# The causal mask of an attention stage: an addition by VectorE, or a product added on TensorE

## The chip, the cores and the metric

The kernel runs on one core of a Trainium2 chip. The metric is the device time of one execution in microseconds (us), taken as the median over several runs. The engines are named as the profile names them: PE is TensorE's matrix multiplication, PEld its weight load, DVE is VectorE, ACT is ScalarE, POOL is GpSimd, and SP is the engine that only issues transfers here. They run side by side and wait for each other through semaphores.

## What is computed

The program is two transformer blocks over 1024 positions of width 1024. The first has a retention and an RWKV mixer and a mixture of 32 experts, the second a latent attention, a short convolution, a state space mixer and a gated feed-forward layer. The change touches only the attention of the second block. Cut to that, the reference is

```python
def block(i):                                   # 128 queries, i = 0..7
    start = i * Q_BLOCK
    sc = jnp.einsum("bqhd,bkhd->bhqk", qn, k_nope) + jnp.einsum("bqhd,bkd->bhqk", qr, k_rope)
    sc = sc.astype(jnp.float32) * scale
    causal = (start + jnp.arange(Q_BLOCK))[:, None] >= key_idx[None, :]
    p = jax.nn.softmax(jnp.where(causal, sc, -jnp.inf), axis=-1)
    return jnp.einsum("bqhk,bkhd->bqhd", p.astype(v.dtype), v)
```

with 8 heads, queries and keys of 96 elements (64 and 32 rotary ones), and values of 64. All of it is float32.

## The kernel before

The program is a row of stages. Each stage has an instruction list of its own for every engine, written out by hand, and ends in a barrier of all engines. `attention_stage` stands between the mixers' stage and the feed-forward stage.

A **step** m is one head and one block i of 128 queries, against the i + 1 blocks of keys that it may see. There are 64 steps. Four steps make a group: the small block i and the large block 7 - i, for each of two heads (u = 0, 1), in the order small u0, large u0, small u1, large u1. Four groups (i = 0 to 3) finish a pair of heads, and the stage has 16 groups. A small step has 1 to 4 blocks of keys, a large one 5 to 8.

In each step:

- PE makes the scores (line 3270) into PSUM: one product of up to 512 columns for a small step, two for a large one. In a profile each float32 product is two records, one for each pass.
- DVE adds the mask `future` (0, and -1e30 right of the diagonal) to the last 128 columns of the scores, in place (line 3358), takes the largest of each row (line 3362), and makes the bias of the exponential from it (line 3366).
- ACT takes the exponential and its sum (line 3323).
- PE turns the result block by block (line 3278, with the identity `ident`; one record each), into the same PSUM banks.
- DVE (small, line 3373) or ACT (large, line 3331) copies the turned blocks to SBUF. After that the banks are free for the scores four steps later.

For each pair of steps of a class, DVE takes the reciprocal of the sums (line 3379), POOL spreads it (line 3259), PE turns it (line 3286), ACT copies that (line 3338), PE multiplies by the values (line 3296, two heads side by side in the array), and DVE multiplies both (line 3385).

PE's order is written out: at step m it makes `scores(m + 2)`, then, where m % 4 is 0 (large class) or 3 (small class), `turn_shares`, then `turn(m)`, and then at those same steps `weigh`. PE waits for the bank in `scores`, for the exponential in `turn`, and for ACT's copy in `weigh`. DVE's order at step m is `shares_of` (m % 4 of 2 or 3), `bound(m + 2)`, `small_out`, `finish`. ACT's order is the copy of the shares, `exps(m + 1)`, and `large_out(m)` for a large step.

The mask comes by a transfer of 64 KB, the first that SP issues in the stage (line 3248). Semaphore `const` tells of it, and DVE waits for it ahead of its first step. `ident` has been in SBUF since the program's start.

Of the kernel before, what the change touches and what calls it, by code (L numbers as in the profile page):

```python
# [10 lines left out]
ALU = mybir.AluOpType  # L11
# [4 lines left out]
P = 128  # L16
# [4 lines left out]
BANK = 512  # L21
# [82 lines left out]
def three(ap, a):  # L104
    return ap.rearrange("p (a b) -> p a b", a=a)
# [2303 lines left out]
def wide(psum, b, n):  # L2409

    return psum[:, b:b + n, :].rearrange("p a b -> p (a b)")
# [780 lines left out]
def attention_stage(nc, psum, bank, ident, a, q_t, k_t, values, feat, late):  # L3192
# [14 lines left out]
    with Stage(nc, "attention") as st:  # L3207
        future = st.sb("future", [P, P])
# [3 lines left out]
        total, share = ([st.sb(f"{n}{c}", [P, 2]) for c in range(2)] for n in ("total", "share"))  # L3212
        spread = [st.sb(f"spread{c}", [P, 2, V_DIM]) for c in range(2)]
        factor = [st.sb(f"factor{c}", [P, P]) for c in range(2)]
        const, scored, masked, most_ready, bias_ready, exp_ready, turned = (
            st.sem(n) for n in "const scored masked most_ready bias_ready exp_ready turned".split())
        p_t_out, share_ready, spread_ready, shares_turned, shares_copied, made, out_done = (
            [st.sem(f"{n}{c}") for c in range(2)] for n in (
                "p_t_out", "share_ready", "spread_ready", "shares_turned", "shares_copied", "made", "out_done"))
# [2 lines left out]
        def of(m):  # L3222


            group, r = m // 4, m % 4
            c, u = r % 2, r // 2
            i = group % HALF
            return group, c, u, (i, TT - 1 - i)[c]

        def head(m):  # L3230
            return m // (4 * HALF) * 2 + of(m)[2]

        def of_class(m):

            return m // 2 + 1

        def score_bank(c, u):
            return (u, 2 + 2 * u)[c]

        def summed(c):  # L3240
            return bank[6 + c][:, 0:P]

        def shares(c):
            return bank[6 + c][:, 2 * P:3 * P]

        @block.sync
        def _(sp):
            sp.dma_start(future[:], a["c_future"]).then_inc(const, 16)
            for n in range(2 * late.halves):
                late.load(sp, n)  # L3250
# [10 lines left out]
        @block.tensor  # L3261
        def _(pe):
            def scores(m):
                group, c, u, i = of(m)
                if group:
                    pe.wait_ge(p_t_out[c], of_class(m - 4))
                h = head(m)
                for n in range(i // 4 + 1):
                    width = min(BANK, (i + 1) * P - n * BANK)
                    last = pe.matmul(bank[score_bank(c, u) + n][:, 0:width], q_t[:, h, i * P:(i + 1) * P],  # L3270
                                     k_t[:, h, n * BANK:n * BANK + width], start=True, stop=True)
                last.then_inc(scored, 1)

            def turn(m):
                group, c, u, i = of(m)
                pe.wait_ge(exp_ready, m + 1)
                for b in range(i + 1):
                    last = pe.transpose(bank[score_bank(c, u) + b // 4][:, (b % 4) * P:(b % 4 + 1) * P],
                                        p[c][u][:, b * P:(b + 1) * P], ident[:])
                last.then_inc(turned, 1)  # L3280

            def turn_shares(group, c):
                if group:
                    pe.wait_ge(out_done[c], group)
                pe.wait_ge(spread_ready[c], group + 1)
                pe.transpose(shares(c), spread[c][:].rearrange("p u d -> p (u d)"), ident[:]).then_inc(shares_turned[c], 1)

            def weigh(group, c):
                m = 4 * group + 2 + c
                i = of(m)[3]  # L3290
                pe.wait_ge(p_t_out[c], of_class(m))
                pe.wait_ge(shares_copied[c], group + 1)
                for b in range(i + 1):
                    for u in range(2):
                        h = group // HALF * 2 + u
                        last = pe.matmul(summed(c)[u * V_DIM:(u + 1) * V_DIM, :], values[:, b, h * V_DIM:(h + 1) * V_DIM],
                                         p_t[c][u][:, b, :], start=(b == 0), stop=(b == i))
                last.then_inc(made[c], 1)

            scores(0)  # L3300
            scores(1)
            for m in range(STEPS):
                if m + 2 < STEPS:
                    scores(m + 2)
                now = (m // 4, SMALL) if m % 4 == 3 else (m // 4 - 1, LARGE) if m % 4 == 0 and m else None
                if now:
                    turn_shares(*now)
                turn(m)
                if now:
                    weigh(*now)  # L3310
            turn_shares(GROUPS - 1, LARGE)
            weigh(GROUPS - 1, LARGE)
# [39 lines left out]
        @block.vector  # L3352
        def _(v):
            def bound(m):
                group, c, u, i = of(m)
                at = wide(psum, score_bank(c, u), 1 + c)
                v.wait_ge(scored, m + 1)
                v.tensor_tensor(at[:, i * P:(i + 1) * P], at[:, i * P:(i + 1) * P], future[:], ALU.add).then_inc(masked, 1)
                v.wait_ge(masked, m + 1)
                if group:  # L3360
                    v.wait_ge(bias_ready, m - 3)
                v.tensor_reduce(most[c][u][:], at[:, 0:(i + 1) * P], AX_X, ALU.max).then_inc(most_ready, 1)
                v.wait_ge(most_ready, m + 1)
                if group:
                    v.wait_ge(exp_ready, m - 3)
                v.tensor_scalar(bias[c][u][:], most[c][u][:], -scale, None, ALU.mult).then_inc(bias_ready, 1)

            def small_out(m):
                group, c, u, i = of(m)
                v.wait_ge(turned, m + 1)  # L3370
                if group:
                    v.wait_ge(made[c], group)
                v.tensor_copy(p_t[c][u][:, 0:i + 1, :], three(bank[score_bank(c, u)][:, 0:(i + 1) * P], i + 1)).then_inc(p_t_out[c], 1)

            def shares_of(group, c):
                v.wait_ge(exp_ready, 4 * group + 3 + c)
                if group:
                    v.wait_ge(spread_ready[c], group)
                v.reciprocal(share[c][:], total[c][:]).then_inc(share_ready[c], 1)

            def finish(group, c):
                i = of(4 * group + 2 + c)[3]
                v.wait_ge(made[c], group + 1)
                v.wait_ge(shares_copied[c], group + 1)
                v.tensor_tensor(feat[:, group // HALF, i * P:(i + 1) * P], summed(c), factor[c][:], ALU.mult).then_inc(out_done[c], 1)

            v.wait_ge(const, 16)
            bound(0)
            bound(1)
            for m in range(STEPS):  # L3390
                group, r = m // 4, m % 4
                if r >= 2:
                    shares_of(group, r - 2)
                if m + 2 < STEPS:
                    bound(m + 2)
                if r % 2 == SMALL:
                    small_out(m)
                if r < 2 and m >= 4:
                    finish(group - 1, r)
            for c in (SMALL, LARGE):  # L3400
                finish(GROUPS - 1, c)
            for c in (SMALL, LARGE):
                v.wait_ge(out_done[c], GROUPS)
# [1227 lines left out]
```

## Time and profile before

| | |
|---|---|
| median of 3 runs | 2931.61 us (2923.81 to 2934.85) |
| the profiled execution, its own time | 2934.81 us |
| its span, first to last instruction | 2933.1 us |
| attention stage, from the first scores to the last DVE operation | 1986.2 to 2141.7 us of the span |
| busy share of the whole span | PE 93%, PEld 76%, DVE 66%, ACT 46%, POOL 20% |

The span is what the profile shows; 1.7 us of the execution's own time lie around it. The busy times are shares of the whole program, in which the attention stage is about a twentieth. What a change in this stage is worth has to be read from rows of this stage.

### The profile page before, as it was taken

The numbers are of one execution on the slowest core, as the hardware profiler recorded it, in microseconds if no ns is written. First come the engines' busy times: TensorE is split into PE (matmuls) and PEld (weight loads), VectorE is DVE, ScalarE is ACT, GpSimd is POOL, SyncE is SP. The second block draws the span as 40 slices with busy tenths as digits, with TensorE's granted clock in tenths as the row PEclk, the third lists the DMA queues.
The fourth block names the chain that finished last, engine by engine and source line by source line (L and its number), as shares of the span: only waits on it lengthen the run. The fifth ranks groups of instructions, "written<-read, shape, count | busy, mean of one in ns | idle before, by whom it ended". The sixth has DMA issues, their size and how long they took to land. (4 is left out here: it accounts for less than half of the span.)

```text
span 2933.1 us, 38735 instructions
## 1 busy us (share of the span) xinstructions
PE 2713.9 (93%) x14472; PEld 2238.9 (76%) x14473; DVE 1935.1 (66%) x2426; ACT 1350.0 (46%) x1898; POOL 580.4 (20%) x489
## 2 busy tenths in 40 slices
PE   8999988989988789999999699879999899999998
PEld 7988777777776668888888588656678688888887
DVE  4441167777764579999998652675678888887314
ACT  5111145555542267777777342235555333334212
POOL 0000036554550110000000420230000233431000
PEclk9999989999999889999999799999999999999999
DMA  6446211111007469999997621001031222222414
GB/s 208 176 181 247 98 39 53 36 36 36 27 16 248 158 259 409 409 410 410 409 411 313 202 76 50 7 1 59 1 95 58 72 85 75 83 86 104 144 47 158
DMA packets 165245, 439.31 MB, mean 150 GB/s; under 512 B 21836, under 2 KB 101760, under 8 KB 151808
## 3 DMA queue, kind: packets, MB, share of 16 engines
q1 hardware_dynamic: 150512, 383.60, 35.5%
q0 software_dynamic: 8848, 33.03, 3.0%
q10 hardware_dynamic: 5760, 20.97, 1.7%
q8 instruction: 83, 1.36, 0.2%
q14 instruction: 42, 0.34, 0.0%
HBM read 358.40 MB, written 79.17 MB: 149 GB/s over the span
## 5 line engine op out<-in xcount | busy, mean ns | idle before, releaser
L134 PE MATMUL psum<-part,expert_x_high 128*128 128x512 f32 x520 | 206.9, 398 | 2.9 <-issue 1.5
L136 PE MATMUL psum<-part,expert_x_low 128*128 128x512 f32 x520 | 203.2, 391 | 0.0
L134 PE MATMUL psum<-project_w_high,high 128*128 128x448 f32 (+1 forms) x512 | 194.6, 380 | 3.5 <-DVE low L398 3.5
L136 PE MATMUL psum<-project_w_high,low 128*128 128x448 f32 (+1 forms) x512 | 193.5, 378 | 0.0
L135 PE MATMUL psum<-project_w_low,high 128*128 128x448 f32 (+1 forms) x512 | 193.5, 378 | 0.0
L129 DVE TENSOR_TENSOR expert_down_low<-expert_down,expert_down_high 128x2048 fp32r<-128x2048 f32 x62 | 139.3, 2289 | 39.6 <-ACT expert_down_high L124 39.6
L971 POOL TENSOR_TENSOR mix_ab_step<-mix_abrb,mix_pair_mask 128x512 f32<-128x512 f32 x80 | 115.6, 1468 | 187.3 <-ACT mix_abrb L1106 186.8
L134 PE MATMUL psum<-part,ffn_w_high 128*128 128x512 f32 x352 | 140.1, 398 | 12.4 <-DVE ffn_w_low L129 7.0
L129 DVE TENSOR_TENSOR expert_gate_low<-expert_gate,part 128x2048 fp32r<-128x2048 f32 x64 | 143.9, 2289 | 8.5 <-ACT part L124 7.1
L129 DVE TENSOR_TENSOR expert_up_low<-expert_up,part 128x2048 fp32r<-128x2048 f32 x64 | 143.8, 2289 | 1.0 <-ACT part L124 1.0
L135 PE MATMUL psum<-ffn_b_low,ffn_w_high 128*128 128x512 f32 x352 | 138.9, 395 | 0.0
L124 ACT ACTIVATE expert_down_high<-expert_down 128x2048 fp32r<-128x2048 f32 x62 | 115.4, 1909 | 19.4 <-ACT expert_y L2167 19.4
L792 DVE TENSOR_TENSOR mix_x_t<-mix_x_t,psum 128x512 f32<-128x512 f32 (+1 forms) x96 | 60.6, 641 | 96.3 <-PE psum L1277 77.2
L124 ACT ACTIVATE part<-expert_gate 128x2048 fp32r<-128x2048 f32 x64 | 119.5, 1921 | 7.6 <-DMA h_rows<-out_xs 7.6
L136 PE MATMUL psum<-down_w_high,ffn_hidden_low 128*128 128x512 f32 x312 | 121.4, 389 | 0.0
L124 ACT ACTIVATE part<-expert_up 128x2048 fp32r<-128x2048 f32 x64 | 119.4, 1924 | 0.0
L134 PEld LDWEIGHTS psum<-part,expert_x_high 128*128 128x128 f32 x520 | 98.2, 189 | 24.4 <-issue 1.8
L136 PEld LDWEIGHTS psum<-part,expert_x_low 128*128 128x128 f32 x520 | 97.9, 188 | 22.0
L4282 POOL TENSOR_TENSOR ffn_sums<-ffn_w 128x512 f32<-128x512 f32 x19 | 38.8, 2042 | 369.5 <-DMA ffn_w<-in_ffn_w_up_dram 369.5
L134 PEld LDWEIGHTS psum<-project_w_high,high 128*128 128x128 f32 x512 | 96.5, 189 | 18.0 <-DVE low L398 4.2
L136 PEld LDWEIGHTS psum<-project_w_high,low 128*128 128x128 f32 x512 | 96.5, 188 | 13.9
L135 PEld LDWEIGHTS psum<-project_w_low,high 128*128 128x128 f32 x512 | 96.6, 189 | 13.5
(701 smaller groups left out, 7598.8 us busy)
## 6 DMA issues: line engine op xcount, KB each, us to landing
expert_gate<-in_w_gate_dram SPq DMA_DIRECT2D x32, 2048.0 KB, 10.2
expert_up<-in_w_up_dram SPq DMA_DIRECT2D x32, 2048.0 KB, 10.1
expert_down<-in_w_down_dram SPq DMA_DIRECT2D x32, 2048.0 KB, 10.8
ffn_w<-in_ffn_w_up_dram SPq DMA_DIRECT2D x44, 512.0 KB, 4.6
y_rows<-expert_y ACTq DMA_DIRECT2D x32, 512.0 KB, 11.0
hidden_rows<-ffn_hidden SPq DMA_DIRECT2D x20, 512.0 KB, 2.8
ffn_hidden<-hidden_rows SPq DMA_DIRECT2D x20, 512.0 KB, 4.0
down_w<-in_ffn_w_down_dram SPq DMA_DIRECT2D x39, 256.0 KB, 2.8
```

The lines of the kernel that those rows point to most:

```text
L124: return act.activation(high, x, ACT.Copy)
L129: return v.tensor_tensor(low, x, high, ALU.subtract)
L134: pe.matmul(out, left[0], right[0], start=start, stop=False)
L135: pe.matmul(out, left[0], right[1], start=False, stop=False)
L136: return pe.matmul(out, left[1], right[0], start=False, stop=stop)
L792: v.tensor_tensor(to, to, by, ALU.add).then_inc(x_ready, 1)
L971: pool.tensor_tensor(ab_step[gr][s % 3][:], abrb[gr][:, :, 0, :], per_block(pair_mask[s + 1][:], HG), ALU.mult).then_inc(ab_split, 1)
L4282: pool.tensor_tensor(s1, a21, a22, ALU.add).then_inc(summed[c], 1)
```

## The change

DVE's addition and its semaphore `masked` go. PE adds the mask itself: behind the scores of each step it multiplies the identity (as weights) with `future` (128 columns, moving), and accumulates onto the 128 columns of the diagonal block. The step's semaphore `scored` is raised by this product. The wait for the mask's transfer moves from DVE's start to PE, behind the scores of step 0.

```diff
-        const, scored, masked, most_ready, bias_ready, exp_ready, turned = (
-            st.sem(n) for n in "const scored masked most_ready bias_ready exp_ready turned".split())
+        const, scored, most_ready, bias_ready, exp_ready, turned = (
+            st.sem(n) for n in "const scored most_ready bias_ready exp_ready turned".split())
...
                 for n in range(i // 4 + 1):
                     width = min(BANK, (i + 1) * P - n * BANK)
-                    last = pe.matmul(bank[score_bank(c, u) + n][:, 0:width], q_t[:, h, i * P:(i + 1) * P],
-                                     k_t[:, h, n * BANK:n * BANK + width], start=True, stop=True)
-                last.then_inc(scored, 1)
+                    pe.matmul(bank[score_bank(c, u) + n][:, 0:width], q_t[:, h, i * P:(i + 1) * P],
+                              k_t[:, h, n * BANK:n * BANK + width], start=True, stop=n < i // 4)
+                if not m:
+                    pe.wait_ge(const, 16)
+                at = i % 4 * P
+                pe.matmul(bank[score_bank(c, u) + i // 4][:, at:at + P], ident[:], future[:], start=False, stop=True).then_inc(scored, 1)
...
                 v.wait_ge(scored, m + 1)
-                v.tensor_tensor(at[:, i * P:(i + 1) * P], at[:, i * P:(i + 1) * P], future[:], ALU.add).then_inc(masked, 1)
-                v.wait_ge(masked, m + 1)
...
-            v.wait_ge(const, 16)
             bound(0)
             bound(1)
```

On PE the list grows by one row in each of the 64 steps. This is the head of the stage, with the difference marked; one row is one product, L3278 and L3281 are the same transposes under the old and the new line number.

```order
 L3270 MATMUL psum<-k_t,q_t 128x128
+L3275 MATMUL psum<-attention_future,ident 128x128
 L3270 MATMUL psum<-k_t,q_t 128x512 x2
+L3275 MATMUL psum<-attention_future,ident 128x128
 L3270 MATMUL psum<-k_t,q_t 128x128
-L3278 MATMUL psum<-ident,attention_p 128x128
+L3275 MATMUL psum<-attention_future,ident 128x128
+L3281 MATMUL psum<-ident,attention_p 128x128
 L3270 MATMUL psum<-k_t,q_t 128x512 x2
```

Every scores product or pair of them is now followed by a mask product, also where the next instruction used to be a transpose of an earlier step.

On DVE the list of before has, at the head of the stage, for steps 0 to 2:

```order
L3358 TENSOR_TENSOR psum<-psum,attention_future 128x128
L3362 TENSOR_REDUCE attention_most<-psum 128x1
L3366 TENSOR_SCALAR attention_bias<-attention_most 128x1
L3358 TENSOR_TENSOR psum<-psum,attention_future 128x128
L3362 TENSOR_REDUCE attention_most<-psum 128x1
L3366 TENSOR_SCALAR attention_bias<-attention_most 128x1
L3358 TENSOR_TENSOR psum<-psum,attention_future 128x128
L3362 TENSOR_REDUCE attention_most<-psum 128x1
L3366 TENSOR_SCALAR attention_bias<-attention_most 128x1
```

and the list of the changed kernel, at the same place, for the same steps:

```order
L3363 TENSOR_REDUCE attention_most<-psum 128x1
L3367 TENSOR_SCALAR attention_bias<-attention_most 128x1
L3363 TENSOR_REDUCE attention_most<-psum 128x1
L3367 TENSOR_SCALAR attention_bias<-attention_most 128x1
L3363 TENSOR_REDUCE attention_most<-psum 128x1
L3367 TENSOR_SCALAR attention_bias<-attention_most 128x1
```

Nothing else moves: the reduction of each step follows directly on the wait for its scores.

## Rows read from the trace of the kernel before

**Rows 1.** The page's part 1: busy us, share of the span, instructions, by engine.
```profile
PE 2713.9 (93%) x14472; PEld 2238.9 (76%) x14473; DVE 1935.1 (66%) x2426; ACT 1350.0 (46%) x1898; POOL 580.4 (20%) x489
```

**Rows 2.** Stretches of the stage: length, busy us (instructions) by engine, granted clock, DMA.
```profile
core 0: us, PE busy (x) PEld busy (x) DVE busy (x) ACT busy (x) POOL busy (x), PEclk, DMA share, GB/s
...
2000.00:2050.00 50.00, 47.91 (x376) 33.25 (x375) 32.00 (x95) 27.93 (x65) 2.94 (x10) 1.00 0.01 2
2050.00:2100.00 50.00, 48.26 (x359) 33.19 (x358) 33.10 (x99) 27.71 (x63) 3.23 (x11) 1.00 0.01 1
```

**Rows 3.** Waits of 1985 to 2140 us, of DVE, PEld and PE: total, times, longest.
```profile
DVE psum L3358 <- PE psum L3270: 47.4, 39, 2.7
...
PEld psum L3270 <- ACT attention_p_t L3331: 6.3, 11, 0.9
...
PEld psum L3278 <- ACT attention_p L3323: 0.6, 1, 0.6
...
PE psum L3296 <- ACT attention_factor L3338: 2.0, 7, 0.3
```

**Rows 4.** Timeline, 2067 to 2076 us: start, length, engine, line, operation [idle before].
```profile
2067.79 0.19 PEld L3270 LDWEIGHTS psum<-k_t,q_t 96*128 96x128 f32 x1 [0.24 <-issue]
2068.22 0.19 PEld L3270 LDWEIGHTS psum<-k_t,q_t 96*128 96x128 f32 x1 [0.24 <-issue]
...
2069.95 0.60 PE L3270 MATMUL psum<-k_t,q_t 96*128 96x256 f32 x2
2070.15 1.02 ACT L3331 ACTIVATE attention_p_t<-psum 128x1024 f32<-128x1024 f32 x1 [2.84 <-PE psum L3278]
2070.39 0.27 PE L3278 MATMUL psum<-ident,attention_p 128*128 128x128 f32 x1
...
2071.23 0.30 PEld L3270 LDWEIGHTS psum<-k_t,q_t 96*128 96x128 f32 x2 [0.91 <-ACT attention_p_t L3331]
...
2072.07 0.20 ACT L3323 ACTIVATION_READ_ACCUMULATOR attention_p<-psum,attention_bias 128x1 f32 x1
...
2072.95 1.03 PE L3278 MATMUL psum<-ident,attention_p 128*128 128x128 f32 x8
...
2074.82 0.27 PE L3286 MATMUL psum<-ident,attention_spread 128*128 128x128 f32 x1
```

**Rows 5.** Timeline of PE, 2058.5 to 2061.5 us: a 128-column product and what follows.
```profile
2060.41 0.39 PE L3270 MATMUL psum<-k_t,q_t 96*128 96x128 f32 x2
2060.63 0.60 PE L3278 MATMUL psum<-ident,attention_p 128*128 128x128 f32 x4
```

**Rows 6.** Groups by form, 1985 to 2140 us: busy us, mean ns | idle before.
```profile
L3270 PE MATMUL psum<-k_t,q_t 96*128 96x128 f32 x32 | 7.1, 306 | 1.9 <-PEq L91 1.9
...
L3358 DVE TENSOR_TENSOR psum<-psum,attention_future 128x128 f32<-128x128 f32 x64 | 18.8, 293 | 54.9 <-PE psum L3270 47.4 <-DMA attention_future<-in_c_future_dram 7.4
```

**Rows 7.** Timeline, the head of the stage, columns as in rows 4.
```profile
1986.16 0.35 SPq L3248 DMA_DIRECT2D attention_future<-in_c_future_dram  x1
...
1986.21 4.61 PE L3270 MATMUL psum<-k_t,q_t 96*128 96x128 f32 x8 [1.86 <-PEq L91]
...
1987.99 0.30 DVE L3358 TENSOR_TENSOR psum<-psum,attention_future 128x128 f32<-128x128 f32 x1 [7.38 <-DMA attention_future<-in_c_future_dram]
```

**Rows 8.** Short stretches of the head, columns as in rows 2.
```profile
1986.00:1988.00 2.00, 1.79 (x4) 1.27 (x5) 0.01 (x1) 1.28 (x1) 0.00 (x0) 0.50 0.28 54
...
1992.00:1994.00 2.00, 2.00 (x4) 0.61 (x4) 1.00 (x5) 1.56 (x4) 0.00 (x0) 0.60 1.04 398
```

**Rows 9.** Timeline, the last steps of the stage, columns as in rows 4.
```profile
2135.21 0.30 DVE L3358 TENSOR_TENSOR psum<-psum,attention_future 128x128 f32<-128x128 f32 x1 [1.35 <-PE psum L3270]
2135.55 0.82 DVE L3362 TENSOR_REDUCE attention_most<-psum 128x1 f32<-128x640 f32 x1
...
2136.70 0.15 DVE L3379 RECIPROCAL attention_share<-attention_total 128x2 f32<-128x2 f32 x1
...
2137.35 0.30 PE L3286 MATMUL psum<-ident,attention_spread 128*128 128x128 f32 x1 [1.19 <-POOL attention_spread L3259]
```

## The prediction, made before the result was known

> **What bounds the kernel now.** The first view is the page's part 1 [rows 1]: PE is busy for 93% of the span. That is a mean over a whole program of which this stage is a twentieth, so the second view is the stretches of this stage [rows 2]. There PE is busy 47.91 of 50 us and 48.26 of 50 us, at the full granted clock, DVE 32.00 and 33.10. PE bounds the stage, with some 4% of its time visibly idle, and DVE has a third of its time free. The third view is who waits for whom [rows 3]. DVE waits 47.4 us for PE's scores, in 39 of 64 steps, and it is the mask addition that sits behind this wait. In the other direction PE's transposes wait once, 0.6 us, for an exponential, the thing that DVE's mask, maximum and bias lead to. So DVE's chain is nearly always early, and an operation taken from it shortens nothing that PE waits for. The fourth view is the timeline [rows 4]: there the exponential's accumulator is read out at 2072.07 to 2072.27 and the transposes that need it start at 2072.95, behind scores that PE streams meanwhile, 0.7 us of slack.
>
> **What is removed.** 64 additions on DVE, 293 ns each, 18.8 us busy [rows 6]. With the handover to the maximum it is 0.34 us a step (2135.21 to 2135.55) [rows 9]. All of it lies beside PE's work, except where PE has nothing left to stream, in the last step. Value on the path: nothing in 63 steps. The cover is the 0.7 us of slack just named; without it 0.34 us a step would be gained.
>
> **What is added.** 64 float32 products of 128 columns, two records each. The trace has just this shape with 96 rows in place of 128: it starts at 2060.41 and the next operation starts at 2060.63 [rows 5], 0.22 us for both records, with PE streaming on either side. Transposes of 128 rows and 128 columns take (2070.39 - 2069.95) / 2 = 0.22 us for one 256-column pass, so 0.11 us per 128 columns, and no row distinguishes 96 from 128 rows. Bounds: below, nothing, where PE would be idle anyway; above, 0.44 us, the 7.1 us busy of the 32 records (16 products) of this shape [rows 6], which counts overlapping ends, exposed weight loads and half-clock passes. I take 0.22, the spacing in a stream, since the mask stands behind a scores product in every step: 64 x 0.22 = 14.1 us.
>
> **What of it is hidden.** PE's weight load for scores waits 11 times, 6.3 us in all, for ACT's copy of a large step's turned blocks [rows 3]. One such wait is in the timeline [rows 4]: the copy starts at 2070.15, as soon as the transposes are through, and ends at 2071.17; PE meanwhile has a small step's scores (2069.95) and one transpose (2070.39), and then idles 0.91 us until 2071.23. The added mask of that small step falls into this very gap, and the release at 2071.17 doesn't depend on it. The mean wait is 0.57 us, and a mask fills 0.22 of it: 11 x 0.22 = 2.4 us hidden. The other repeated wait, that of the products with the values for ACT's copy of the shares (7 times, 2.0 us) [rows 3], hides nothing: the copy is released by PE's own transposition of the shares (2074.82) [rows 4], which comes behind the mask in PE's order and so slides with it.
>
> **The head of the stage.** Now DVE waits for the mask's transfer, issued at 1986.16 and landed at 1987.99, while PE streams on from 1986.21 [rows 7]. After the change PE waits for it, behind the scores of step 0, and behind this wait are queued the mask of step 0, the scores of steps 1 and 2, and with them everything. The scores of step 0 are one product, two passes of 0.22 us at the half clock of these rows (0.50) [rows 8], done near 1986.7. PE idles some 1.3 us. The clock is granted in full only within 1992 to 1994 us (0.60 in that row) [rows 8], after PE has been busy from 1986.21. Idle time at half clock is worth half, 0.65 us, if the full clock comes at the same instant, 1.3 us if it slides along by as much, and near 2.5 us if it comes later still. The middle: 1.3 us. The three or four masks ahead of that instant run at half clock, but they displace other half-clock work, so in that sliding picture they count 0.22 each, already in the sum.
>
> **The tail.** In the last step nothing follows for PE to stream. PE waits at 2137.35 for the spread shares, these for the reciprocal at 2136.70, and this stands in DVE's queue behind mask, maximum and bias of step 63 (2135.21 on) [rows 9]. There 0.34 us leaves the path: -0.3 us.
>
> **Sum.** 14.1 - 2.4 + 1.3 - 0.3 = 12.7 us more, all in this stage. The stages around it start from a barrier and are not touched, so the span grows by as much: 2934.8 + 12.7 = 2947.5 us for an execution like the profiled one. That one is 3.2 us above the median of the three runs, 2931.6, and against the median the forecast is **2944.3 us**, +0.43%.
>
> A rule weighed against this: by the Trainium skill, "Perfetto Trace Analysis", section "Identifying the Most-Contended Engine", a matmul's busy share is a bad measure of PE's headroom, and the share of its weight loads is the one to take. That share is 33.25 of 50 us here [rows 2], so by the rule a third of the stage would be free for the masks. The trace speaks against it where float32 passes stream: one weight load at 2067.79 is followed by the next at 2068.22 [rows 4], 0.43 us for a load of 0.19, because the 512-column pass between them takes 0.43.
>
> **The rivals.**
>
> *Dearer masks (ends slower by over 0.5%).* A weight load that can't run ahead of its pass is added to it. Where a wait held the loads back, two of 0.19 us each take 0.30 us together (2071.23) [rows 4], so one is followed by the next after 0.11 us, and about that much stands in the open ahead of a first pass. If the identity's load were exposed in each mask, or the accumulation onto columns just written cost something like it, a mask would cost 0.33 us. Its place is every step; with 53 unhidden masks the time is 53 x 0.33 + 1.0 = 18.5 us more, 2950.1 us. It decides against my class from 0.26 us a mask on, (14.7 - 1.0) / 53. Against it: the first transposes behind scores, with the same identity as weights, show their load running ahead.
>
> *Nothing hidden, or the clock late.* The waits for ACT's copy may slide with PE after all, or the full clock may come later in the head: 14.1 + 1.3 to 2.5 - 0.3 = 15 to 16.3 us more, near 2947.5 us.
>
> *Masks mostly hidden.* PE's busy time is modelled at its ends, and there may be more room than 4%, as the share of weight loads suggests [rows 2]. If two thirds of the masks fell into it, 14.1 / 3 + 1.0 = 5.7 us more: 2937.3 us.
>
> *DVE's chain is the true limit (ends faster).* If PE's records hid waits for exponentials, each step would lose 0.34 us of DVE and gain 0.22 us of PE: 64 x 0.12 = 7.7 us less, 2923.9 us. This needs the slack of 0.7 us [rows 4] to be absent in most steps, and one wait of 0.6 us [rows 3] speaks against it.
>
> **How the numbers follow.** The forecast, 10 to 14.6 us more, has 57%. Dearer masks 12%, nothing hidden or a late clock 15%, mostly hidden 11%, the chain 5%. The range has to leave out no more than 2 in 10: from 2935 us, which takes in much of "mostly hidden", to 2951 us, which takes in the dearer masks. It leaves out the chain's case, a part of the hidden one, and prices over 0.34 us a mask. About 0.5%, 14.7 us, is what a measurement of this kernel can tell from no change. The forecast lies below that bound by only 2 us. Slower by over 0.5%: the two dearer cases, and a little of the forecast's own spread, 0.29. Faster by over 0.5% would need nearly double what the chain's case gives: 0.02. The rest, 0.69, is within 0.5%.
>
> **What would show it.** In the changed kernel's profile: (1) a group of 128 mask records on PE, and the addition gone from DVE; (2) 0.22 us from the start of a mask to the start of what follows it in a stream; (3) PEld's waits for ACT's copy down from 6.3 us to about 4; (4) PE's scores of step 1 starting near 1988.4 in place of 1986.8, behind a wait for the transfer; (5) DVE's wait for PE grown by about what it lost in work and the stage gained in length, 30 us; (6) the last steps' wait for the spread shares 0.3 us shorter; (7) the stage 12 to 13 us longer, and nothing else longer. The forecast is wrong if the spacing behind a mask is over 0.26 us, if transposes start to wait for exponentials, or if the stages after this one change.

## The result

| | before | after |
|---|---|---|
| median of 9 runs | 2930.48 us (2922.62 to 2934.85) | 2944.64 us (2933.01 to 2948.80) |
| profiled execution, its span | 2933.1 us | 2942.9 us |
| attention stage in it | 155.5 us (1986.2 to 2141.7) | 167.8 us (1983.8 to 2151.6) |

The ratio is 1.0049, with a 95% interval of 1.0032 to 1.0066: the changed kernel is slower, by 14.2 us in the medians (the interval is 9.4 to 19.3 us), against 12.7 us forecast. Whether that is more or less than 0.5%, nine runs of each don't decide, since the interval holds both.

The profile says more than the total. The stage itself is 12.3 us longer. In this pair of executions it also began 2.4 us earlier, though nothing ahead of it was changed, and what lies behind it took 791.4 us before and 791.3 us after. So the two spans differ by only 9.8 us.

The page after, its span and part 1:

```profile
span 2942.9 us, 38926 instructions
...
PE 2724.0 (93%) x14600; PEld 2251.0 (76%) x14601; DVE 1922.1 (65%) x2362; ACT 1347.6 (46%) x1898; POOL 581.1 (20%) x489
```

PE has 128 instructions more than in [rows 1], DVE 64 fewer. The shares move by a point at most, which is why they can't judge a change in one stage of the program.

The best yardstick here is the middle of the stage. Its order of work repeats every four groups (16 steps), and a stretch of just that length, after the first and up to the third such round, is the same to a hundredth of a microsecond in both executions of each kernel. Such a stretch is called a round below. Its length, busy time by engine, clock and DMA, in the kernel before and then in the kernel after:

```profile
core 0: us, PE busy (x) PEld busy (x) DVE busy (x) ACT busy (x) POOL busy (x), PEclk, DMA share, GB/s
2033.67:2071.25 37.58, 36.00 (x273) 24.78 (x273) 24.45 (x74) 20.84 (x49) 2.35 (x8) 1.00 0.00 1
2035.53:2075.98 40.45, 39.36 (x304) 28.92 (x304) 20.09 (x58) 20.41 (x49) 2.35 (x8) 1.00 0.00 1
```

A round has grown by 2.87 us. Sixteen masks of 0.22 us are 3.52 us, thirteen are 2.86 us: three of sixteen were hidden, as forecast. The waits of the stage after, PEld's, PE's and DVE's, total, times, longest:

```profile
PEld psum L3270 <- ACT attention_p_t L3334: 3.0, 8, 0.6
PEld psum L3275 <- DMA attention_future<-in_c_future_dram: 1.5, 1, 1.5
...
PEld psum L3281 <- ACT attention_p L3326: 0.2, 1, 0.2
...
PE psum L3299 <- ACT attention_factor L3341: 2.0, 7, 0.3
...
DVE attention_most L3363 <- PE psum L3275: 83.8, 52, 7.9
```

Against [rows 3]: the waits for ACT's copy of the turned blocks fell from 6.3 us in 11 to 3.0 us in 8. The waits for its copy of the shares stayed at 2.0 us in 7, to the tenth. DVE waits for PE 75.9 us beside the one wait of 7.9 us at the head, up from 47.4. Line by line, one of the waits that shrank and a mask in the stream (timeline after):

```profile
1994.12 0.60 PE L3270 MATMUL psum<-k_t,q_t 96*128 96x256 f32 x2
...
1994.32 1.02 ACT L3334 ACTIVATE attention_p_t<-psum 128x1024 f32<-128x1024 f32 x1 [1.10 <-PE psum L3281]
...
1994.56 0.39 PE L3275 MATMUL psum<-attention_future,ident 128*128 128x128 f32 x2
...
1994.78 0.27 PE L3281 MATMUL psum<-ident,attention_p 128*128 128x128 f32 x1
...
1995.40 0.30 PEld L3270 LDWEIGHTS psum<-k_t,q_t 96*128 96x128 f32 x2 [0.58 <-ACT attention_p_t L3334]
```

The mask starts at 1994.56 and what follows it at 1994.78: 0.22 us. ACT's copy runs from 1994.32 to 1995.34 beside it, and the wait that was 0.91 us in [rows 4] is 0.58 us. All mask products of the stage after, as a group by form:

```profile
L3275 PE MATMUL psum<-attention_future,ident 128*128 128x128 f32 x128 | 25.6, 282 | 1.3 <-DMA attention_future<-in_c_future_dram 1.3
```

25.6 us "busy" for work that lengthens PE's stream by 14: the ends of records overlap. Priced by busy time, the forecast would have been nearly twice too high. The head of the stage after:

```profile
1983.78 0.35 SPq L3248 DMA_DIRECT2D attention_future<-in_c_future_dram  x1
...
1983.82 0.46 PE L3270 MATMUL psum<-k_t,q_t 96*128 96x128 f32 x2 [1.97 <-PEq L91]
...
1985.54 0.80 PE L3275 MATMUL psum<-attention_future,ident 128*128 128x128 f32 x2 [1.26 <-DMA attention_future<-in_c_future_dram]
...
1986.13 3.62 PE L3270 MATMUL psum<-k_t,q_t 96*128 96x512 f32 x4
```

PE has its first product done, waits 1.26 us for the transfer, and comes to the scores of step 1 only 2.3 us into the stage. In this execution the clock was still granted in full for the first 0.9 us of the stage (1983.82 to 1984.74), where the forecast had it at half. The tail after:

```profile
2145.36 0.82 DVE L3363 TENSOR_REDUCE attention_most<-psum 128x1 f32<-128x640 f32 x1 [1.91 <-PE psum L3275]
2145.91 0.70 ACT L3334 ACTIVATE attention_p_t<-psum 128x640 f32<-128x640 f32 x1 [2.31 <-PE psum L3281]
...
2147.16 0.30 PE L3289 MATMUL psum<-ident,attention_spread 128*128 128x128 f32 x1 [0.86 <-POOL attention_spread L3259]
```

The wait for the spread shares is 0.86 us, 0.33 less than in [rows 9].

### The profile page after: what moved, and what is told of

Same layout as the page of the kernel before. It is cut to its first block and busy times, and to the rows that moved or that the text cites. A ratio compares the mean times of both kernels' runs of the same rounds, so it can differ in the third digit from the quotient of the medians.

```text
span 2942.9 us, 38926 instructions
## 1 busy us (share of the span) xinstructions
PE 2724.0 (93%) x14600; PEld 2251.0 (76%) x14601; DVE 1922.1 (65%) x2362; ACT 1347.6 (46%) x1898; POOL 581.1 (20%) x489
```

## Experiments

Each kernel's stage was measured in its profile. Kernels without a ratio were run once, and only their profiles are used. "Round" is four groups in the middle; "head" runs from the first scores to the end of the eighth output of DVE; "at half" is the time in the stage's first 20 us during which the granted clock was 0.50; "tail" runs from the start of PE's last scores record to the end of the stage.

| kernel | mask on | stage | head | at half | round | tail | ratio to before (95%) |
|---|---|---|---|---|---|---|---|
| before | DVE | 155.5 | 47.5 | 7.4 | 37.58 | 6.78 | |
| before, again | DVE | 155.3 | 47.3 | 6.8 | 37.58 | 6.78 | |
| after | PE | 167.8 | 51.7 | 6.8 | 40.45 | 6.76 | 1.0049 (1.0032 to 1.0066) |
| after, again | PE | 167.8 | 51.8 | 6.8 | 40.45 | 6.76 | |
| both | PE and DVE | 168.1 | 52.2 | 6.8 | 40.45 | 7.00 | |
| none | nobody | 154.5 | 46.4 | 4.0 | 37.58 | 6.54 | |
| in the gap | PE in 15 steps | 155.1 | 46.5 | 3.4 | 37.80 | 6.78 | |
| outside the gap | PE in 15 steps | 158.4 | 47.9 | 5.8 | 38.46 | 6.78 | |
| doubled | PE, twice | 179.0 | 54.7 | 5.8 | 43.44 | 6.99 | 1.0073 (1.0052 to 1.0094) |
| late first masks | PE | 165.1 | 49.1 | 3.4 | 40.45 | 6.76 | 1.0047 (1.0028 to 1.0066) |
| late, bfloat16 | PE | 158.6 | 48.2 | 6.8 | 38.39 | 6.60 | 1.0006 (0.9993 to 1.0019) |
| shares first | DVE | 151.0 | 45.2 | 3.4 | 36.74 | 6.78 | 0.9984 (0.9972 to 0.9996) |
| shares first, copy cut | DVE | 149.0 | 45.6 | 6.9 | 35.94 | 6.78 | 0.9980 (0.9968 to 0.9993) |

### Is DVE's relief worth anything? Both, and none

Theory: PE's stream sets the stage. Rival: DVE's chain does, and a part of the price was paid back by its relief. The first kernel gives DVE its addition back and keeps PE's product, so the mask is added twice:

```diff
                 v.wait_ge(scored, m + 1)
+                v.tensor_tensor(at[:, i * P:(i + 1) * P], at[:, i * P:(i + 1) * P], future[:], ALU.add).then_inc(masked, 1)
+                v.wait_ge(masked, m + 1)
```

> PE adds the mask as in the changed kernel and DVE adds it as well (the diagonal block gets it twice). Theory (PE's stream sets the stage, DVE's chain is covered): the stage is as long as in the changed kernel, 167.8 us, plus the 0.3 us of the tail, so 168.1 us, and four groups in its middle take 40.4 us as there. Rival (DVE's chain is the limit and its relief pays a part of the change back): some 0.3 us in each of 64 steps comes on top, up to 188 us, and four groups take over 42 us.

The second is the kernel before without the two lines and without anything in their place; it leaves out the mask.

> Nobody adds the mask (the computation leaves it out, so the weights reach into future positions), DVE is relieved and PE is as before. Theory: only the tail gains, the stage is 155.2 us against 155.5 before, and four groups in the middle take 37.6 us as before. Rival (DVE's chain): up to 0.34 us less in each step that waits, four groups under 36 us.

A round of each, columns as above:

```profile
2026.57:2067.02 40.45, 39.36 (x305) 28.93 (x305) 24.51 (x74) 20.82 (x49) 2.35 (x8) 1.00 0.00 1
```

```profile
2030.59:2068.17 37.58, 36.00 (x272) 24.79 (x272) 20.02 (x59) 20.42 (x49) 2.35 (x8) 1.00 0.01 1
```

DVE's busy time in a round is 24.51 us in the first and 20.09 in the kernel after, and the round is 40.45 us in both. It is 20.02 us in the second and 24.45 before, and the round is 37.58 us in both. The rival is dead: 4.4 us of DVE a round are worth nothing. Only the tail differs, by 0.24 us in either pair (7.00 to 6.76, 6.78 to 6.54), where 0.3 was expected. The column "head" ends with an operation of DVE, so it holds 0.34 us of DVE's work as well: on PE itself the products ahead of that end start within 0.13 us of each other in the first kernel and the two executions of the kernel after.

That the second's stage, 154.5 us, is below the 155.2 expected lies in its head, which had 3.4 us less at half clock. On PE the head is only 0.8 us shorter for it: with the full clock this early PE catches up with DVE and ACT and waits 0.7 us for the exponential of step 1, where PE itself had no such wait before:

```profile
PE psum L3278 <- ACT attention_p L3323: 0.7, 1, 0.7
```

### Are masks hidden in the wait for ACT's copy? In the gap, and outside it

PE takes the mask in 15 steps only, the rest stays on DVE; this is the kernel in the gap, the other has `m % 4 == 1`:

```diff
+        def on_pe(m):
+            return m >= 4 and m % 4 == 0
...
```

> PE adds the mask in 15 steps alone, the small ones of the first head from the second group on (m of 4 is 0), whose scores stand between a large step's transposes and the scores that wait for ACT's copy of them; DVE adds it in the other 49. Theory: where PE waited for ACT (i of 0, 1 and 3 at the large step) the mask is hidden, in every fourth group it is not: 3 to 4 x 0.22 = 0.7 to 0.9 us more than before, a stage of 156.3 us, four groups 37.8 us. Rival (the waits slide with PE, nothing is hidden): 15 x 0.22 = 3.3 us more, 158.8 us, four groups 38.5 us.

> PE adds the mask in 15 other steps, the large ones of the first head from the second group on (m of 4 is 1), whose scores stand behind the wait for ACT's copy; DVE in the other 49. Theory: nothing hides these, 15 x 0.22 = 3.3 us more than before, 158.8 us, four groups in the middle 37.58 + 0.87 = 38.4 us. Rival (any idle time of PE takes them up): as for the small steps, under 156.5 us.

The rounds, the one in the gap first:

```profile
2027.87:2065.67 37.80, 36.71 (x281) 25.86 (x281) 23.47 (x70) 20.82 (x49) 2.35 (x8) 1.00 0.01 1
```

```profile
2036.15:2074.61 38.46, 36.88 (x281) 25.81 (x281) 23.25 (x71) 20.81 (x49) 2.35 (x8) 1.00 0.01 1
```

Four masks a round cost 0.22 us in the gap, which is one of them, and 0.88 us outside it, which is all four. PEld's waits for ACT's copy in the stages of the two:

```profile
PEld psum L3273 <- ACT attention_p_t L3339: 3.0, 8, 0.6
```

```profile
PEld psum L3273 <- ACT attention_p_t L3339: 6.3, 11, 0.9
```

In the gap they fall just as in the kernel after, outside it they stay as before. So the 3 hidden of 16 are these small steps and no others. The stages are 155.1 us for 156.3 expected, with 4.0 us less at half clock in the head, and 158.4 for 158.8, with 1.7 us less; in both PE waits for the exponential of step 1 as above (0.5 and 0.2 us), so the clock gives back less than half of these lengths.

### What does one product cost? Doubled

```diff
+                pe.matmul(bank[score_bank(c, u) + i // 4][:, at:at + P], ident[:], future[:], start=False, stop=False)
                 pe.matmul(bank[score_bank(c, u) + i // 4][:, at:at + P], ident[:], future[:], start=False, stop=True).then_inc(scored, 1)
```

> The mask product of the changed kernel is issued twice in each step. Theory (0.22 us a product in the stream; what was left of the waits for ACT's copy, 3.0 us in 8 waits, takes up a little): 64 x 0.22 = 14.1 us, less up to 2 us, so a stage of 179.9 to 181.9 us, four groups 43.6 us, and the whole kernel 12 to 14 us above the changed one, 1.009 of the kernel before. Rival (a mask behind a mask of the same columns waits for the accumulation, or exposes a weight load): 0.33 us or more each, 189 us.

A round, and two masks in a row with what they show of the spacing:

```profile
2036.64:2080.08 43.44, 42.58 (x338) 32.45 (x336) 20.18 (x58) 20.43 (x49) 2.37 (x8) 1.00 0.01 2
```

```profile
2052.24 0.39 PE L3275 MATMUL psum<-attention_future,ident 128*128 128x128 f32 x2
2052.46 0.39 PE L3276 MATMUL psum<-attention_future,ident 128*128 128x128 f32 x2
```

0.22 us from mask to mask, on the very columns just written, so accumulation costs nothing and no weight load is exposed. A round is 2.99 us longer than after. 16 x 0.22 = 3.52, and the remaining waits for ACT's copy took 0.5 us of it, some 2 us over the stage. The stage, 179.0 us, is 0.9 us below the range, with 1.0 us less at half clock than in the kernel after, worth half a microsecond. The whole kernel is 1.0073 of before; the 1.009 expected lies inside its interval.

### The head: late first masks

```diff
-                if not m:
-                    pe.wait_ge(const, 16)
+                if m > 1:
+                    mask(m)
...
             scores(0)
             scores(1)
+            pe.wait_ge(const, 16)
+            mask(0)
+            mask(1)
```

> The changed kernel, with the masks of steps 0 and 1 both behind the scores of step 1, so that the wait for the mask's transfer stands behind 3.4 us of products. Theory: the 1.3 us of idle PE at the head go, the stage is 166.3 to 167.1 us against 167.8, middle unchanged (four groups 40.45 us). Rival (the head's cost is the later grant of the full clock for another reason, or none at all): 167.8 us.

The stage is 2.6 us shorter, more than the 0.7 to 1.5 us expected. PE's waits name no transfer any more; the load of the first mask shows 0.52 us behind products that PE is still streaming:

```profile
1982.75 0.33 PEld L3278 LDWEIGHTS psum<-attention_future,ident 128*128 128x128 f32 x1 [0.52 <-DMA attention_future<-in_c_future_dram]
```

The head, from the first scores to the eighth output, as a stretch, with its mean granted clock:

```profile
1980.65:2029.73 49.08, 47.96 (x338) 34.56 (x338) 23.89 (x67) 24.45 (x56) 2.37 (x8) 0.97 0.25 88
```

1.7 us of the difference are the clock: the head of this execution had 3.4 us at half clock, that of the kernel after 6.8. While PE streams, each such stretch costs half its length: in the kernel after, the four passes of step 1's scores (1986.13 to 1989.55) take 0.86 us each at half clock, and 0.43 us is what such a pass takes at the full clock [rows 4]. PE streams through this stretch in both kernels. 0.9 us are left for the pause. Whether the missing pause also shortened the time at half clock this run can't say, since the kernels that have no pause either show anything from 3.4 to 7.4 us. By the times, 1.0047 against 1.0049, the two kernels aren't told apart: the gain is shown by the stage alone, and its size only after a correction for the clock.

### Is it PE's passes? bfloat16

As the last one, with the product's operands cast once at the head:

```diff
+            v.tensor_copy(ident_b[:], ident[:]).then_inc(cast, 1)
+            v.wait_ge(const, 16)
+            v.tensor_copy(future_b[:], future[:]).then_inc(cast, 1)
...
-                pe.matmul(bank[score_bank(c, u) + i // 4][:, at:at + P], ident[:], future[:], start=False, stop=True).then_inc(scored, 1)
+                pe.matmul(bank[score_bank(c, u) + i // 4][:, at:at + P], ident_b[:], future_b[:], start=False, stop=True).then_inc(scored, 1)
```

> As the one with the late masks, but identity and mask are cast to bfloat16 by DVE at the head, so that the mask is one record of 128 columns in place of two float32 ones. Theory (what is paid is PE's passes): at most half, 0.11 us a mask, as a float32 transpose of one record takes, so four groups at 37.58 + 16 x 0.11 - 0.3 = 39.0 us or less, the stage near 162 us; if the pass streams faster than its weight load, no less than 38.3 us. Rival (the cost is one of switching, of the semaphore or of the accumulation, whatever the passes): 40.4 us as with float32.

```profile
2021.94:2060.33 38.39, 36.99 (x288) 25.28 (x288) 20.02 (x59) 20.40 (x49) 2.35 (x8) 1.00 0.01 1
```

```profile
2035.99 0.22 PE L3280 MATMUL psum<-attention_future_b,attention_ident_b 128*128 128x128 bf16 x1
2036.05 0.28 PE L3294 MATMUL psum<-ident,attention_spread 128*128 128x128 f32 x1
```

The mask is now 0.06 us in the stream, and a round is 0.81 us above before: 13 unhidden masks of 0.06 us. That is less than the 0.11 us that was the most expected, and the stage is 158.6 us where some 162 was. The same accumulation at the same place in the order costs a quarter: the price is that of the passes. The kernel is 1.0006 of before, its interval holding 1. By whole runs a mask on PE in this form can't be told from one on DVE; by the round it costs 0.81 us.

### What the reading is good for: shares first, and the copy cut

The forecast told two kinds of repeated waits apart: one that a mask fills, and one that slides with PE's own order. The second should go when that order changes, with the mask left on DVE:

```diff
+                now = (m // 4, SMALL) if m % 4 == 3 else (m // 4 - 1, LARGE) if m % 4 == 0 and m else None
+                if now and now[1] == LARGE:
+                    turn_shares(*now)
                 if m + 2 < STEPS:
                     scores(m + 2)
-                now = (m // 4, SMALL) if m % 4 == 3 else (m // 4 - 1, LARGE) if m % 4 == 0 and m else None
-                if now:
+                if now and now[1] == SMALL:
                     turn_shares(*now)
```

> The kernel before (mask on DVE), with one order changed on PE: the transposition of the large class's shares is issued ahead of the next small step's scores in place of behind them. Theory (that wait, for ACT's copy of the shares, is set by where PE itself issues the transposition, so it slides with what stands ahead and hides nothing): the products with the values no longer wait in 15 groups, 0.2 to 0.5 us each and the exposed load with them, four groups at 37.58 - 1.4 = 36.2 us, the stage 5 us shorter, 150.5 us, the kernel 0.998 of before. Rival (ACT's queue sets it, ACT being busy with the large copy): under 1 us.

```profile
2028.91:2065.65 36.74, 35.68 (x273) 24.54 (x273) 24.43 (x75) 20.77 (x49) 2.37 (x8) 1.00 0.00 1
```

A round is 0.84 us shorter and not 1.4, the kernel 0.9984 of before. The stage, 151.0 us, comes near the 150.5 expected only by luck: its head had 4.0 us less at half clock than that of the kernel before. The mechanism holds: no wait of PE for ACT's copy of the shares is left in the view of this stage up to its last steps. The size was off, by a fixed pause that I had counted as waiting, as a piece of the timeline shows:

```profile
2067.79 0.60 PE L3278 MATMUL psum<-ident,attention_p 128*128 128x128 f32 x4
...
2068.32 0.44 PE L3296 MATMUL psum<-attention_p_t,values 128*64 128x128 f32 x4
...
2068.69 0.33 PE L3286 MATMUL psum<-ident,attention_spread 128*128 128x128 f32 x1
...
2068.86 0.60 PE L3270 MATMUL psum<-k_t,q_t 96*128 96x256 f32 x2
```

The four transposes take 0.43 us of stream (4 x 0.108) and end at 2068.22; the products with the values start at 2068.32, although nothing holds them. The 0.10 us is there at each change between products over the full and over half the array's width, here before and behind L3296. That part of the 0.2 to 0.5 us could not be won, and at i of 0 and 1 a wait of 0.2 us for ACT's copy of the turned blocks remains. The transposition also takes 0.17 us in its new place, for 0.11 in a stream.

The last kernel adds to this a cut of ACT's copy into one for each PSUM bank, so that the scores can start on the first (PE's waits are counted to match, which is left out here):

```diff
...
-                act.activation(p_t[c][u][:, 0:i + 1, :], three(wide(psum, score_bank(c, u), 2)[:, 0:(i + 1) * P], i + 1), ACT.Copy)\
-                    .then_inc(p_t_out[c], 1)
+                for n, blocks in enumerate((range(0, 4), range(4, i + 1))):
+                    first, last = blocks[0], blocks[-1] + 1
+                    act.activation(p_t[c][u][:, first:last, :], three(bank[score_bank(c, u) + n][:, 0:(last - first) * P], last - first), ACT.Copy)\
+                        .then_inc(p_t_out[c], 1)
```

> The kernel before (mask on DVE), with the large class's shares turned first as in the run before, and ACT's copy of a large step's turned blocks cut in two, one for each PSUM bank, so that the first scores product waits for the first bank's copy alone. Theory: the waits for ACT's copy, 6.3 us in 11, in which a mask product could hide, end some 0.4 us earlier each, 3 to 4 us in all; four groups at 36.74 - 0.9 = 35.8 us, the stage 147 us, the kernel 0.997 of before. Rival (ACT loses by 32 more instructions of some 0.2 us what PE gains, or the second bank's copy is late in its turn): four groups at 36.5 us or more.

```profile
2032.31:2068.25 35.94, 35.49 (x273) 24.52 (x272) 24.39 (x74) 21.14 (x57) 2.37 (x8) 1.00 0.01 1
```

A round is 35.94 us (35.8 expected) with 35.49 of it busy, and the kernel is 0.9980 of before (0.997 expected), faster than both kernels of this case. The stage is 149.0 us where 147 was expected; a part of the miss is the head, which had 3.5 us more at half clock than that of the kernel before it in the table. Times alone don't tell these last two apart; their rounds do.

### The head and the start again

> The kernel before, a further execution, for the head of the stage and the start of it. Theory: four groups in the middle take 37.58 us again to the hundredth; the stage's start moves by microseconds with the granted clock ahead of it (1973.7 to 1988.2 us so far), and its head (to the second head pair's results) by up to 1.7 us with the instant of the full clock, without the kernel being another. Rival (the stage's length is as steady as its middle): 155.5 us and a head of 47.46 us.

> The changed kernel, a further execution. Theory: middle 40.45 us for four groups, the idle time of PE ahead of the first mask 1.3 us again, and a head above that of an execution of the kernel before by 3.3 us of masks, 1.3 us of idle time at half clock (worth 0.65) and what the full clock comes later. Rival (the wait shifts nothing since the full clock comes at an instant of its own): head 4.0 us above the other at most.

The heads of the two, from the first scores to the eighth output, columns as above:

```profile
1979.58:2026.89 47.31, 45.14 (x297) 29.82 (x297) 29.55 (x87) 25.18 (x57) 2.37 (x8) 0.93 0.26 91
```

```profile
1982.33:2034.08 51.75, 49.29 (x338) 35.25 (x338) 23.93 (x67) 24.45 (x56) 2.37 (x8) 0.93 0.23 83
```

Rounds of 37.58 and 40.45 us again (to the hundredth, within rounding), and stages of 155.3 and 167.8 us. Both heads had 6.8 us at half clock. The kernel before scattered less than was expected: its head is 47.3 us for 47.5, with 0.6 us less at half clock, which is nearer to the rival.

The heads differ by 4.44 us, more than the 4.0 us of the rival, and not by a later full clock either, since the time at half clock is equal. The eighth output ends behind step 19, where DVE gets its 0.34 us back and PE pays one mask more. Just ahead of that, at the products with the values, PE is 4.54 us later than in the kernel before. It has issued 19 masks by then, 3 of them in the gap, so 16 x 0.22 = 3.5 us are masks, and 1.0 us are left for the pause, against 0.9 us by the kernel with the late first masks. The pause itself, with the clock:

```profile
1982.33 0.46 PE L3270 MATMUL psum<-k_t,q_t 96*128 96x128 f32 x2 [1.96 <-PEq L91]
1984.12 0.79 PE L3275 MATMUL psum<-attention_future,ident 128*128 128x128 f32 x2 [1.34 <-DMA attention_future<-in_c_future_dram]
```

```profile
1982.33:1983.27 0.94, 0.45 (x2) 0.26 (x2) 0.00 (x0) 0.94 (x1) 0.00 (x0) 1.00 0.00 2
1983.27:1984.12 0.85, 0.00 (x0) 0.00 (x0) 0.00 (x0) 0.30 (x1) 0.00 (x0) 0.50 0.72 124
```

PE idles for 1.34 us (the rows give its end, 1984.12, and length). The clock was granted in full until 1983.27, so 0.49 us of it pass at the full clock and 0.85 us at half, worth 0.49 + 0.85 / 2 = 0.9 us.

## Why the prediction was right

The forecast was 12.7 us. The stage grew by 12.3 us, which is what the sum was about. The medians grew by 14.2 us; that they came within 1.5 us of the forecast, with runs that scatter by 12 us and more, is in part luck.

- **What bounds the kernel.** PE's stream, with DVE's chain covered. Shown by the kernel with both: DVE's 4.4 us a round change nothing.
- **Price of a mask, 0.22 us.** Right, in the kernel after (1994.56 to 1994.78) and from mask to mask in the doubled one. That 128 rows cost what 96 do was assumed, and is shown by it: the prediction's working for transposes of 128 rows, (2070.39 - 2069.95) / 2, is taken from a scores product of 96 rows [rows 4].
- **Hidden, 11 of 64.** Right as to which: 3 a round, shown by the kernels in and outside the gap. The mean wait of 0.57 us was read rightly as more than a mask, and the doubled kernel found what was left of it. The weight load's waits fell further than forecast, to 3.0 us and not about 4: three waits less, 3.3 us in all, of which 11 x 0.22 = 2.4 us are masks in PE's stream, as the rounds show.
- **The shares' wait hides nothing.** Right: 2.0 us in 7 before and after.
- **Head, 1.3 us between 0.65 and 2.5.** The pause was 1.26 and 1.34 us in two executions. Its price was 0.9 to 1.0 us, by two ways: two executions with equal time at half clock, and the kernel that covers the pause. So the middle was 0.3 to 0.4 us too high. I had put the whole pause at half clock and let the full clock slide along with it; in both executions the pause began at the full clock, and in the pair compared the full clock didn't slide. That it might in others is not excluded: the time at half clock came and went by 4 us among the kernels.
- **Tail, 0.34 us.** 0.24 us measured. The wait for the shares shrank by the 0.33 us forecast. The rest of the chain behind it didn't follow wholly: the last transposes wait for an exponential on ACT, and ACT is still at its copy of the turned blocks, whose record ends at 2146.61. The exponential starts at 2146.51, where its bias is there from 2146.37; before it followed its bias within 0.03 us. The kernel in which nobody adds the mask shows the same 0.14 us, so it doesn't come from PE's mask.
- **Sum.** 53 x 0.22 = 11.7, + 1.0 - 0.2 = 12.5 us, for 12.3 us in the first pair of executions, where the kernel before had 0.6 us more at half clock, and 12.5 in the second, where the two had the same.
- **The rule of the Trainium skill on the share of weight loads** ("Perfetto Trace Analysis", section "Identifying the Most-Contended Engine") would have had a third of the stage free (33.25 of 50 us in [rows 2]). The trace doesn't agree. A round had 37.58 - 36.00 = 1.58 us of PE idle, hid 0.66 us of masks, and lengthened by the rest. The measurement decides for the busy share, in this stage of float32 passes.
- **Rivals.** Dearer masks fell with the spacing of 0.22 us. Nothing hidden fell with the kernel in the gap. Masks mostly hidden and DVE's chain fell with the rounds. What is left open is whether the kernel is slower by over 0.5%: at +0.49% the time sits on that bound. I gave "slower" 0.29, fair for a forecast 2 us below a bound with runs that scatter by 12.

## What to carry to other kernels

Moving work from an engine with slack to the one that bounds the stage cost its full spacing in that engine's stream, less only what fell into waits whose release doesn't depend on the moved work; a wait whose release comes from behind it in the same queue slid along and hid nothing. Both can be told apart in the trace of the kernel before. Price an operation by the distance between starts in a stream, not by its busy time (here 0.22 against 0.40 us a mask), and look for a repeating round in the trace to check it: it showed 0.22 us where whole runs scatter by 12. The two kinds of wait also say what to do: the sliding one wants its cause issued sooner, the other a release in smaller pieces.

## What the runs showed of the hardware

The same instructions ahead of the stage bring it to its start anywhere between 1973.7 and 1988.2 us. These are the kernels of the two ends (bfloat16 and outside the gap), from the program's first products to the stage, columns as above:

```profile
17.00:1973.00 1956.00, 1781.56 (x10004) 1490.97 (x10002) 1298.38 (x1489) 961.05 (x1288) 422.78 (x371) 0.96 0.47 182
```

```profile
17.00:1988.00 1971.00, 1799.41 (x10007) 1506.92 (x10005) 1297.35 (x1489) 961.43 (x1288) 423.63 (x371) 0.95 0.47 181
```

DVE, ACT and POOL are busy for the same time in both; PE is busy 18 us longer in the second, at a granted clock of 0.95 for 0.96. So this scatter, as large as the change's effect, goes along with the clock granted in the stages ahead, and not with the kernels' difference, which lies behind them. Why the clock differs no run shows.

A bfloat16 mask of 128 columns stands 0.06 us in the stream and a float32 one 0.22 us, and both accumulate onto float32 scores. For the float32 one this adds nothing that shows: the product of the same columns that accumulates nothing stands 0.22 us in the stream as well [rows 5]. Where products over the full width of the array and products over half of it follow each other, the spacing is 0.20 us and not 0.11, 0.10 us more each way; no run varies the width alone, so that it is the cause is argued only.
